# GpSimd instead of SyncE issues the reads that bring regrouped token tiles back, in a gated convolution and neighbourhood attention encoder

## The chip, the cores and the metric

One core of one Trainium2 chip. The metric is the device time of one execution in microseconds (us), lower is better. The kernel before took 1714.12 us, the median of 3 runs (1713.75 to 1716.57).

## The reference

One encoder layer and a final RMSNorm for two requests with the same weights, 512 and 1024 tokens of 1024 channels, all in float32. The part that the change touches is the first two lines.

```python
def _layer(x, norm_g, w_in, b_gate, dw_w, dw_b, ln_g, ln_b, w_pw_a, rpb, w_o_b, w_out):
    proj = _rmsnorm(x, norm_g) @ w_in
    a_val, a_glu, z_a, q, k, v, z_b, g_logits = jnp.split(proj, np.cumsum(sizes)[:-1].tolist(), axis=-1)
    y_a = (_conv_module(a_val, a_glu, dw_w, dw_b, ln_g, ln_b) * jax.nn.silu(z_a)) @ w_pw_a
    attn = _neighbourhood_attention(q.reshape(hs), k.reshape(hs), v.reshape(hs), rpb)
    y_b = (attn * jax.nn.silu(z_b)) @ w_o_b
    gates = jax.nn.sigmoid(g_logits + b_gate)
    merged = gates[..., :D_MODEL] * y_a + gates[..., D_MODEL:] * y_b
    return x + merged @ w_out
```

## The kernel before

The 1536 tokens are 12 tiles of 128. Every float32 operand of a matrix product is split into a high and a low part, and each product is three passes on TensorE (PE in the profile). The normalised and transposed activations stay in SBUF as `xs` (high and low), the weights come piece by piece.

**The first phase** (up to about 83 us) does two things at once. It normalises and transposes the 12 tiles, and it multiplies each finished tile with the first half of the V weights: one group of 24 matmuls per tile (`token_group`, the matmul of L1675). PE works through the tiles in order, so tile t has to be in `xs` when the group of tile t - 1 ends. After that come the conv groups (L1657), the other V half, Q and K, and the attention units, all with `xs` complete.

How a tile gets into `xs`:

- SyncE (SP) loads it (`load_x`, L502); ScalarE squares and sums it (`square`, L843); VectorE scales the sum (`mean_square_x`, L1221); GpSimd (POOL) takes the power -1/2 (L729), in a loop over the 12 tiles, each behind a wait for `ms_ok`.
- Tiles 0 to 4: VectorE multiplies (`normalise`, L1235), PE transposes (`h_t`, L1695).
- Tiles 5 to 11 (from `SHUFFLED`) leave PE alone: VectorE multiplies and turns the tile in blocks of 32 x 32 (`turn`, four of L1246 and the transpose L1249, into one of two buffers `xn`), and SP moves the blocks through DRAM (`shuffle_x`): four stores to `x_d` (L521), a wait until they have landed, one read of 512 KB back into `xt` (L523).
- All tiles: ScalarE copies the high part (`h_hi`, L858, two halves; for tiles 5 to 11 it waits for the read by `x_back`), VectorE subtracts for the low part (`h_lo`, L1261, two halves), and `x_lo` lets PE go on.

ScalarE's program has `h_hi(t + 1)` ahead of `take_v(t)`, which empties PE's group t (L871) and issues its store (L874). VectorE's has `h_lo(t)` ahead of `turn(t + 3)`.

**SP's order** in `shuffle_x`, in one queue: tile 5 before the load of tile 11, then tiles 6 to 11, then the window masks (L532), the small parameters (L535, into the buffer of the odd `xn`) and the weight pieces of the second V half (L494).

**The semaphores**: `xr_ok` counts the turned tiles, `x_out` the stores (64 for a tile), `x_back[t % 2]` the reads (16 each). `turn(t)` waits on `x_out` until the stores of tile t - 2, which used the same buffer, are done.

**GpSimd after the loop** waits for the whole `xs` (`x_lo` at 24), clears a small table, loads the position bias and writes it as a shifted table to DRAM (L735, L739: 16 DMAs), then builds the masked biases (L759) that attention takes.

Of the kernel before, what the change touches and what calls it, by code (L numbers as in the profile page):

```python
# [104 lines left out]
SHUFFLED = 5  # L105
# [86 lines left out]
def build(nc, x_prompt, x_sample, norm_g, w_in, b_gate, dw_w, dw_b, ln_g, ln_b, w_pw_a, rpb,  # L192
          w_o_b, w_out, final_g, masks, y_prompt, y_sample):
    with ExitStack() as ctx:
# [3 lines left out]
        def sem(name):  # L198
            return ctx.enter_context(nc.semaphore(name))

        def scratch(name, shape):
            return nc.dram_tensor(name, shape, F32, kind="Internal").ap()
# [30 lines left out]
        xt = work[:, 0:8 * D].rearrange("p (s d) -> p s d", s=8)  # L233
# [33 lines left out]
        def wt(s, part):  # L267

            return spare[:, part, :] if wslot(s) == X_SLOT else ws[:, wslot(s), part, :]
# [43 lines left out]
        x_d = scratch("x_d", [NT, P, 4, 2 * P])  # L313
# [12 lines left out]
        table0, rel_out = sem("table0"), sem("rel_out")  # L326
        mask_ok, pads_ok = sem("mask_ok"), sem("pads_ok")
        sq_ok, ms_ok, rstd_ok, xn_ok, ht_ps = (sem(n) for n in ("sq_ok", "ms_ok", "rstd_ok", "xn_ok", "ht_ps"))
        xp_ok, xr_ok, x_out, x_back = sem("xp_ok"), sem("xr_ok"), sem("x_out"), [sem(f"x_back{i}") for i in range(2)]
        x_hi, x_lo, x0_hi, x0_lo = sem("x_hi"), sem("x_lo"), sem("x0_hi"), sem("x0_lo")  # L330
        w_ld = [sem(f"w_ld{i}") for i in range(2)]
        w_ld2 = [sem(f"w_ld2{i}") for i in range(2)]
# [51 lines left out]
        def w_rows(w, col, s):  # L384

            return w.rearrange("(k p) c -> p k c", p=P)[:, 2 * s:2 * s + 2, col:col + CH]
# [28 lines left out]
        def grs(g):  # L415

            return g % 2, g + 1, g // 2 + 1
# [61 lines left out]
        def after(eng, sm, count):  # L479

            if not isinstance(count, int) or count > 0:
                eng.wait_ge(sm, count)
# [5 lines left out]
        def _(sp):  # L488
# [26 lines left out]
            def shuffle_x(t):  # L515

                sp.wait_ge(xr_ok, t - SHUFFLED + 1)
                spot = x_d[t].rearrange("(g i) a n -> a i g n", g=4)
                for a in range(4):
                    src = xn[t % 2][32 * a:32 * a + 32, :].rearrange("p (g n) -> p g n", g=4)  # L520
                    sp.dma_start(spot[a], src).then_inc(x_out, 16)  # L521
                sp.wait_ge(x_out, 64 * (t - SHUFFLED + 1))
                sp.dma_start(xt[:, t % 8, :], x_d[t].rearrange("p a n -> p (a n)")).then_inc(x_back[t % 2], 16)  # L523

            for t in range(8, NT):
                load_x(t)
# [1 line left out]
                    shuffle_x(t - 5)  # L528
            for t in range(7, NT):
                shuffle_x(t)  # L530
            sp.wait_ge(w_lo, 4)
            sp.dma_start(msk32, masks).then_inc(mask_in, 16)  # L532
            for r, n, src in ((0, TAPS, dw_w[0]), (I_DWB, 1, dw_b[0:1, :]), (I_LNG, 1, ln_g[0:1, :]),
# [135 lines left out]
            for e in range(2 * 24):  # L669
                ct, n = (e % 24) // NCH, e % NCH  # L670
                if e >= 3:

                    b, _, out = grs(G_YB + e - 3)
# [19 lines left out]
            for j in range(6, 8):  # L693
                src = w_rows(w_out[0], CH, j - 4)
# [7 lines left out]
            for e in range(4, 2 * NT):  # L702
                b, _, out = grs(G_OUT + e - 4)
# [10 lines left out]
        @block.gpsimd  # L714
        def _(pool):
            nc.gpsimd.memset(ident[:], 0.0).then_inc(const_ok, 1)
            nc.gpsimd.memset(half, -0.5).then_inc(const_ok, 1)
            pool.wait_ge(const_ok, 2)
            nc.gpsimd.affine_select(out=ident[:], in_=ident[:], compare_op=ALU.not_equal, fill=1.0, base=0,
                                    pattern=[[-1, P]], channel_multiplier=1).then_inc(const_ok, 1)  # L720
            for t in range(NT):
                if t == 1:

                    pool.wait_ge(w_hi, 1)
                    pool.wait_ge(xn_ok, 2)
                    nc.gpsimd.tensor_tensor(wt(0, 1), raw_of(0), wt(0, 0).bitcast(F32), ALU.subtract).then_inc(w_lo, 1)

                pool.wait_ge(ms_ok, t + 1)
                nc.gpsimd.tensor_tensor(rstd[:, t:t + 1], ssq[:, t:t + 1], half, ALU.pow).then_inc(rstd_ok, 1)  # L729

            pool.wait_ge(x_lo, 3 * KT)
            nc.gpsimd.memset(table[0:HEADS, :], 0.0).then_inc(table0, 1)
            pool.wait_ge(table0, 1)
            t3 = table[0:HEADS, :].rearrange("h (r c) -> h r c", r=RROWS)
            pool.dma_start(t3[:, 4:4 + 15, 16:16 + 31], rpb[0]).then_inc(tab_in, 16)  # L735
            pool.wait_ge(tab_in, 16)
            for c in range(QB):

                pool.dma_start(rel_d[:, c, :, :], t3[:, :, 15 - c:15 - c + ECOLS]).then_inc(rel_out, 16)  # L739
            pool.wait_ge(mask_ok, 1)  # L740

            def unit(i):
                for kd in range(KINDS):
                    for h in range(2):
                        s, jk = kd // 3, kd % 3
                        j = JKIND.index(jk)
                        nk = SEG_ROWS[s] * 8 * QUADS[j]
                        if kd == 0:
                            pool.wait_ge(e_in[h], 128 * i + 128)

                        used = 0 if kd < 2 else blk(0, 4 * ((kd - 2) // 3) + [0, 2, 3][(kd - 2) % 3], h)
                        after(pool, t_ok, 24 * i + used)
                        e0 = 16 - QB * j + BAND_START[j]
                        e = et[h][:, SEG_E0[s]:SEG_E0[s] + SEG_ROWS[s], e0:e0 + 8 * QUADS[j]]
                        if QUADS[j] == 3:
                            e, w = e.rearrange("p r (v w) -> p v r w", v=3), 8
                        else:
                            e, w = e.rearrange("p (c g) w -> p g c w", g=4), BAND
                        nc.gpsimd.tensor_tensor(  # L759
                            bt[:, 2 * (kd % 2) + h, 0:nk].rearrange("p (g c w) -> p g c w", g=QUADS[j], w=w),  # L760
                            mask[:, KIND_OFF[kd]:KIND_OFF[kd] + nk].rearrange("p (g c w) -> p g c w", g=QUADS[j], w=w),
                            e, ALU.subtract).then_inc(bias_ok, 1)

            unit(0)
            with pool.Fori(1, PAIRS) as i:
                unit(i)


            pool.wait_ge(c_out, 32 * PAIRS)
            for k in range(KT):  # L770

                pool.wait_ge(x_lo, 5 * KT + k + 1 if k < KT - 2 else 6 * KT)
                if k >= 3:
                    pool.wait_ge(dev, k - 2)
                pool.dma_start(cs[:, k, :], c_d[k]).then_inc(c_in[k], 16)

            pool.wait_ge(var_ok, 1)
            nc.gpsimd.tensor_tensor(var, var, half.to_broadcast([P, NT]), ALU.pow).then_inc(rcol_ok, 1)

            def load_za(e):  # L780
                n, k = e // KT, e % KT
                pool.dma_start(tmp3[:, chunk(e % 3)], za_d[k, :, chunk(n)]).then_inc(za_in[e % 3], 16)


            pool.wait_ge(sum_ps, 2 * NCH + 1)
            for n in range(3):
                pool.wait_ge(st_out[n], 128 + 48 * PAIRS)
            for e in range(3):
                load_za(e)
            for e in range(3 * KT):  # L790
                n, k = e // KT, e % KT
                pool.wait_ge(lw, e + 1)
                pool.wait_ge(za_in[e % 3], 16 * (e // 3 + 1))
                nc.gpsimd.tensor_tensor(cs[:, k, chunk(n)], cs[:, k, chunk(n)], tmp3[:, chunk(e % 3)],
                                        ALU.mult).then_inc(ta_ok, 1)
                if e + 3 < 3 * KT:
                    pool.wait_ge(ta_ok, e + 1)
                    load_za(e + 3)

            for t in range(NT):  # L800
                pool.wait_ge(fms, t + 2 + t // (NT - 1))
                nc.gpsimd.tensor_tensor(rsf[:, t:t + 1], rstd[:, t:t + 1], half, ALU.pow).then_inc(frs, 1)
# [399 lines left out]
        def _(dve):  # L1202
# [34 lines left out]
            def turn(t):  # L1237

                dve.wait_ge(rstd_ok, t + 1)
                n = t - SHUFFLED  # L1240
                after(dve, x_out, 64 * (n - 1))
                src = xt[:, t % 8, :].rearrange("p (k g i) -> p k g i", k=KT, g=4)
                dst = xn[t % 2].rearrange("p (g k i) -> p k g i", g=4, k=KT)
                g = ngb.rearrange("p (k g i) -> p k g i", k=KT, g=4)
                for q in range(4):
                    nc.vector.scalar_tensor_tensor(dst[:, :, q, :], src[:, :, q, :], rstd[:, t:t + 1], g[:, :, q, :], ALU.mult,  # L1246
                                                   ALU.mult).then_inc(xp_ok, 1)
                dve.wait_ge(xp_ok, 4 * n + 4)
                nc.vector.transpose(xn[t % 2], xn[t % 2]).then_inc(xr_ok, 1)  # L1249
# [309 lines left out]
            for phase, e0, s0 in ((2, 0, S_YB), (3, 24, S_YA)):  # L1559
                for gi in range(24):  # L1560
                    tile, n = gi // NCH, gi % NCH
# [38 lines left out]
            for e in range(2 * NT):  # L1600
                c, t = e // NT, e % NT
# [4 lines left out]
                b, done, _ = grs(G_OUT + e)  # L1606
# [351 lines left out]
```

## Time and profile before

| | |
|---|---|
| median of 3 runs | 1714.12 us |
| the profiled execution | 1714.49 us |
| its span | 1712.7 us |
| PE busy | 1701.9 us, 99% of the span |
| VectorE busy | 1154.4 us, 67% |
| ScalarE busy | 463.9 us, 27% |
| GpSimd busy | 186.3 us, 11% |
| DMA | 237.57 MB, 139 GB/s on average |

The span is the time from the first to the last instruction; the profiled execution's own time is 1.79 us more. PE is busy nearly all the time, so what matters is how long it waits and where; matmuls are pipelined and their ends are modelled, so that a short wait can hide inside a busy stretch and shows in the spacing of the groups.

### The profile page before, as it was taken

To read this page: it belongs to the slowest core of one execution; us is meant where nothing else is said; L and a number is where in the kernel's file an instruction comes from. 1 tells how busy PE (TensorE), PEld (TensorE's weight loads), DVE (VectorE), ACT (ScalarE), POOL (GpSimd) and SP (SyncE) were. 2 spreads that over 40 slices of the span, in tenths; PEclk is the share of its full clock that TensorE was granted. 3 is DMA by queue.
4 is the path that set the end of the run, shared out by engine and by line. 5 is a ranking of instruction groups with operands and counts; after the bars stand their busy time and mean duration, and the time that the engine had idled before them with its cause. 6 is when DMAs were issued, how large, how long until landed. Compare 5 with 4: busy or idle time off the path is not lost.

```text
span 1712.7 us, 25348 instructions
## 1 busy us (share of the span) xinstructions
PE 1701.9 (99%) x8644; PEld 1404.3 (82%) x8644; DVE 1154.4 (67%) x1875; ACT 463.9 (27%) x931; POOL 186.3 (11%) x251
## 2 busy tenths in 40 slices
PE   9999999999999999999999999999999999999998
PEld 7788888888888888888888888888887888888887
DVE  6549256896798589579678958967986655335332
ACT  5321123223122222222222222231234344003222
POOL 1120011001011001001101100010110064000001
PEclk9999999999999999999999999999999999999999
DMA  8751345444435434534543553453458675643223
GB/s 299 236 95 50 97 122 137 122 118 138 130 88 157 110 106 124 157 90 118 152 122 82 146 138 103 115 146 112 131 149 313 229 223 164 199 130 105 76 91 130
DMA packets 281286, 237.57 MB, mean 139 GB/s; under 512 B 106040, under 2 KB 235080, under 8 KB 281069
## 3 DMA queue, kind: packets, MB, share of 16 engines
q1 hardware_dynamic: 231818, 147.01, 30.7%
q10 hardware_dynamic: 45506, 75.78, 13.3%
q0 software_dynamic: 3872, 13.75, 3.0%
q8 instruction: 38, 0.62, 0.2%
q14 instruction: 52, 0.42, 0.1%
HBM read 152.75 MB, written 83.71 MB: 138 GB/s over the span
## 4 chain that ended last, share of the span: by engine, by line
PE 93%; DMA 3%; DVE 2%; SPq 1%; issue 1%; ACT 0%; ACTq 0%; POOL 0%; POOLq 0%; DVEq 0%
PE pg L1657 74%; PE pg L1675 12%; PE pS L1834 2%; PE pS L1815 2%; DMA x_d<-work 1%; PE pO L1834 1%; PE pO L1815 1%; DMA work<-in_norm_g 1%; DVE xs L1214 1%; SPq L521 0%; DMA work<-p_d 0%; DMA p_d<-work 0%; DMA m_d<-work 0%; PE pS L1792 0%; DMA work<-x_d 0%
## 5 line engine op out<-in xcount | busy, mean ns | idle before, releaser
L1657 PE MATMUL pg<-xs,ws 128*128 128x512 f32 x5688 | 1303.8, 390 | 0.2 <-DVE work L1555 0.2
L1657 PEld LDWEIGHTS pg<-xs,ws 128*128 128x128 f32 x5688 | 1064.1, 188 | 228.2 <-issue 6.4
L1328 DVE SCALAR_TENSOR_TENSOR work<-work 128x1551 f32<-128x1551 f32 x240 | 439.1, 1830 | 16.8 <-issue 12.0
L1675 PE MATMUL pg<-ws,xs 128*128 128x512 f32 x942 | 218.7, 390 | 0.8 <-DVE xs L1261 0.8
L1675 PEld LDWEIGHTS pg<-ws,xs 128*128 128x128 f32 x942 | 176.4, 188 | 38.2 <-issue 1.7
L759 POOL TENSOR_TENSOR work<-work 128x288 f32<-128x288 bf16 (+3 forms) x72 | 53.5, 742 | 976.3 <-DVE small L1401 964.0
L1052 ACT ACTIVATE work<-work,small 128x288 f32<-128x288 f32 (+3 forms) x192 | 102.7, 537 | 200.9 <-DVE small L1401 200.9
L1206 DVE TENSOR_TENSOR ws<-raw,ws 128x1024 fp32r<-128x1024 f32 x88 | 109.2, 1242 | 54.1 <-ACT ws L812 54.1
L812 ACT ACTIVATE ws<-raw 128x1024 fp32r<-128x1024 f32 x89 | 93.9, 1056 | 127.5 <-PE pg L1657 99.2
L1401 DVE CUSTOM_DVE_ANT_0 work<-pS,work 128x384 f32<-128x384 f32 (+3 forms) x128 | 53.3, 463 | 95.7 <-PE pS L1815 94.6
L1413 DVE STREAM_TRANSPOSE work<-work 128x288 f32<-128x288 f32 (+3 forms) x192 | 94.0, 490 | 6.6
L1411 DVE TENSOR_SCALAR work<-work,small 128x288 f32<-128x288 f32 (+3 forms) x192 | 90.1, 469 | 6.8
L1025 ACT ACTIVATE work<-pg,work 128x512 f32<-128x512 f32 x48 | 33.1, 689 | 163.3 <-PE pg L1657 158.7
L1551 DVE SCALAR_TENSOR_TENSOR work<-qk,pg 128x512 f32<-128x512 f32 x24 | 16.5, 687 | 73.0 <-PE pg L1657 73.0
L759 POOL TENSOR_TENSOR work<-work,ws 128x288 f32<-128x288 bf16 (+3 forms) x72 | 56.2, 780 | 68.6 <-DMA ws<-rel_d 68.6
L1625 DVE TENSOR_TENSOR work<-pg,work 128x512 f32<-128x512 f32 x23 | 15.9, 691 | 59.2 <-PE pg L1675 59.2
L1360 DVE TENSOR_TENSOR ws<-pg,qk 128x512 fp32r<-128x512 f32 x24 | 16.5, 689 | 49.4 <-ACT qk L914 49.4
L1214 DVE SCALAR_TENSOR_TENSOR xs<-work,xs 128x512 fp32r<-128x512 f32 x69 | 43.1, 686 | 8.9 <-ACT xs L965 8.9
L914 ACT ACTIVATE qk<-pg 128x512 fp32r<-128x512 f32 x24 | 14.4, 599 | 118.5 <-PE pg L1657 118.5
L1834 PEld LDWEIGHTS pS<-work 128*64 128x64 f32 (+1 forms) x672 | 34.4, 136 | 11.3 <-issue 11.3
L965 ACT ACTIVATE xs<-work 128x512 fp32r<-128x512 f32 x69 | 38.0, 621 | 20.4 <-DVE work L1547 9.1
L920 ACT ACTIVATE qk<-pg 128x512 fp32r<-128x512 f32 x24 | 14.4, 598 | 105.9 <-PE pg L1657 105.9
(142 smaller groups left out, 1023.4 us busy)
## 6 DMA issues: line engine op xcount, KB each, us to landing
raw<-in_w_in SPq DMA_DIRECT2D x70, 512.0 KB, 3.8
p_d<-work SPq DMA_DIRECT2D x128, 96.0 KB, 2.1
work<-p_d ACTq DMA_DIRECT2D x32, 384.0 KB, 3.6
p_d<-work SPq DMA_DIRECT2D x128, 72.0 KB, 1.9
work<-p_d ACTq DMA_DIRECT2D x31, 288.0 KB, 3.7
v_d<-work ACTq DMA_DIRECT2D x24, 256.0 KB, 2.6
work<-v_d SPq DMA_DIRECT2D x64, 96.0 KB
za_d<-work ACTq DMA_DIRECT2D x24, 256.0 KB, 2.1
```

The lines of the kernel that those rows point to most:

```text
L759: nc.gpsimd.tensor_tensor(bt[:, 2 * (kd % 2) + h, 0:nk].rearrange("p (g c w) -> p g c w", g=QUADS[j], w=w), mask[:, KIND_OFF[kd]:KIND_OFF[ ...
L812: nc.scalar.activation(wt(s, 0), raw_of(s), ACT.Copy).then_inc(w_hi, 1)
L1052: nc.scalar.activation(t, t, ACT.Exp, scale=-1.0, bias=mn[:, x:x + 1], accum_out=rsum[:, x:x + 1]).then_inc(p_exp, 1)
L1206: nc.vector.tensor_tensor(wt(s, 1), raw_of(s), wt(s, 0).bitcast(F32), ALU.subtract).then_inc(w_lo, 1)
L1214: nc.vector.scalar_tensor_tensor(xs[:, k, 1, chunk(n)], src_of(k), scale, xs[:, k, 0, chunk(n)].bitcast(F32), ALU.mult, ALU.subtract).then ...
L1328: nc.vector.scalar_tensor_tensor(cv[:, 0:CLEN], u[:, k:k + CLEN], cur[:, k:k + 1], cv[:, 0:CLEN], ALU.mult, ALU.add).then_inc(tap_ok, 1)
L1401: nc.vector.tensor_tensor_reduce(out=head_of(tt, b, h), in0=bank_of(b, h)[:, 0:nk], in1=bt[:, 2 * (kind_of(b) % 2) + h, 0:nk], scale=1.0, ...
L1411: nc.vector.tensor_scalar(t, t, rinv[:, x:x + 1], None, ALU.mult).then_inc(p_ok, 1)
L1413: nc.vector.transpose(t, t).then_inc(tr_done, 1)
L1657: last = nc.tensor.matmul(pg[b][:], wt(s, wpart)[:, k * P:(k + 1) * P], xs[:, k, xpart, chunk(n)], start=(j == 0 and wpart == 1), stop=(j ...
L1675: last = nc.tensor.matmul(pg[b][:], xs[:, k, xpart, t * P:(t + 1) * P], wt(s0 + k // 2, wpart)[:, chunk(k % 2)], start=(k == 0 and xpart = ...
L1834: mm = nc.tensor.matmul(o[:, a:z], vb[0:rows_of(b), SEG_RG[s] + c, j, rows], p[:, c, a:z], start=(n == 0), stop=(n == nc_ - 1))
```

## The change

SP no longer waits for its stores and no longer reads the tiles back. GpSimd does, in its loop over the tiles: after the power of tile 6 it waits for the stores of tile 5 and issues the read of tile 5, and so on by a small table; the reads of tiles 9, 10 and 11 all come after the last power. The stores are counted by two semaphores, for odd and even tiles. New on SP is a wait before the stores of tile t until the read of tile t - 2 has landed, and one for all stores before the masks.

```diff
-        xp_ok, xr_ok, x_out, x_back = sem("xp_ok"), sem("xr_ok"), sem("x_out"), [sem(f"x_back{i}") for i in range(2)]
+        xp_ok, xr_ok, x_out, x_back = sem("xp_ok"), sem("xr_ok"), [sem(f"x_out{i}") for i in range(2)], [sem(f"x_back{i}") for i in range(2)]
...
             def shuffle_x(t):
 
                 sp.wait_ge(xr_ok, t - SHUFFLED + 1)
+                after(sp, x_back[t % 2], 16 * ((t - SHUFFLED) // 2))
...
-                    sp.dma_start(spot[a], src).then_inc(x_out, 16)
-                sp.wait_ge(x_out, 64 * (t - SHUFFLED + 1))
-                sp.dma_start(xt[:, t % 8, :], x_d[t].rearrange("p a n -> p (a n)")).then_inc(x_back[t % 2], 16)
+                    sp.dma_start(spot[a], src).then_inc(x_out[t % 2], 16)
...
+            for i, n in ((0, 3), (1, 4)):
+                sp.wait_ge(x_out[i], 64 * n)
             sp.wait_ge(w_lo, 4)
...
+            def load_back(t):
+
+                pool.wait_ge(x_out[t % 2], 64 * ((t - SHUFFLED) // 2 + 1))
+                pool.dma_start(xt[:, t % 8, :], x_d[t].rearrange("p a n -> p (a n)")).then_inc(x_back[t % 2], 16)
...
                 nc.gpsimd.tensor_tensor(rstd[:, t:t + 1], ssq[:, t:t + 1], half, ALU.pow).then_inc(rstd_ok, 1)
+                for b in {6: (5,), 8: (6,), 9: (7,), 10: (8,), 11: (9, 10, 11)}.get(t, ()):
+                    load_back(b)
...
-                after(dve, x_out, 64 * (n - 1))
+                after(dve, x_out[t % 2], 64 * (n // 2))
```

SP's queue before, from the stores of tile 5 to those of tile 7. `x_d<-work` is a store (4 for a tile), `work<-x_d` the read, `work<-in_x_sample` the load of tile 11.

```order
L521 DMA x_d<-work 32x4x256 [waits xr_ok]
L521 DMA x_d<-work 32x4x256 x3
L523 DMA work<-x_d 128x1024 [waits x_out]
L502 DMA work<-in_x_sample 128x1024 [waits ht_ps]
L521 DMA x_d<-work 32x4x256 [waits xr_ok]
L521 DMA x_d<-work 32x4x256 x3
L523 DMA work<-x_d 128x1024 [waits x_out]
L521 DMA x_d<-work 32x4x256 [waits xr_ok]
```

SP's queue with the change, from the stores of tile 5 to those of tile 8:

```order
L522 DMA x_d<-work 32x4x256 [waits xr_ok]
L522 DMA x_d<-work 32x4x256 x3
L502 DMA work<-in_x_sample 128x1024 [waits ht_ps]
L522 DMA x_d<-work 32x4x256 [waits xr_ok]
L522 DMA x_d<-work 32x4x256 x3
L522 DMA x_d<-work 32x4x256 [waits x_back1,xr_ok]
L522 DMA x_d<-work 32x4x256 x3
L522 DMA x_d<-work 32x4x256 [waits x_back0,xr_ok]
```

The reads and their waits are gone, the load of tile 11 follows the stores of tile 5 at once, and from tile 7 on the stores wait for the read of two tiles before.

GpSimd's program with the change, from the power of tile 1 (the first row is that of tiles 1 to 6) to the clearing of the table:

```order
L735 TENSOR_TENSOR small<-small 128x1 [waits ms_ok] x6
L725 DMA work<-x_d 128x1024 [waits x_out1]
L735 TENSOR_TENSOR small<-small 128x1 [waits ms_ok] x2
L725 DMA work<-x_d 128x1024 [waits x_out0]
L735 TENSOR_TENSOR small<-small 128x1 [waits ms_ok]
L725 DMA work<-x_d 128x1024 [waits x_out1]
L735 TENSOR_TENSOR small<-small 128x1 [waits ms_ok]
L725 DMA work<-x_d 128x1024 [waits x_out0]
L735 TENSOR_TENSOR small<-small 128x1 [waits ms_ok]
L725 DMA work<-x_d 128x1024 [waits x_out1]
L725 DMA work<-x_d 128x1024 [waits x_out0]
L725 DMA work<-x_d 128x1024 [waits x_out1]
```

Before, the eleven powers of tiles 1 to 11 stood in one row with nothing between them; now the powers of tiles 7, 9, 10 and 11 stand behind a read and its wait.

## Rows read from the trace of the kernel before

**Rows 1.** Waits of PE in the whole span: us in total, times, longest us
```profile
PE pg L1702 <- POOL ident L719: 1.6, 1, 1.6
...
PE pg L1675 <- DVE xs L1261: 0.8, 2, 0.5
```
**Rows 2.** PE's L1675, groups of tiles 8 to 11: length, then busy (count)
```profile
59.54:64.98 5.44, 5.40 (x24) 4.13 (x22) 1.00 0.74 238
64.98:70.97 5.99, 5.72 (x24) 4.43 (x24) 1.00 0.70 222
70.97:77.18 6.21, 5.76 (x25) 4.72 (x26) 1.00 0.77 262
77.18:82.67 5.49, 5.45 (x24) 4.13 (x23) 1.00 0.66 248
```
**Rows 3.** ScalarE and PE around tile 10: start us, length us, line [idle before]
```profile
69.91 1.16 ACT L858 ACTIVATE xs<-work 128x512 fp32r<-128x512 f32 x2 [4.33 <-DMA work<-x_d]
...
71.42 11.21 PE L1675 MATMUL pg<-ws,xs 128*128 128x512 f32 x48 [0.52 <-DVE xs L1261]
```
**Rows 4.** SP's DMA issues from 29 to 75 us: start, length
```profile
33.79 0.34 SPq L523 DMA_DIRECT2D work<-x_d  x1
...
46.45 0.34 SPq L523 DMA_DIRECT2D work<-x_d  x1
...
53.58 1.88 SPq L521 DMA_DIRECT2D x_d<-work  x4
59.36 0.34 SPq L523 DMA_DIRECT2D work<-x_d  x1
...
66.07 2.33 SPq L521 DMA_DIRECT2D x_d<-work  x4
71.27 0.34 SPq L523 DMA_DIRECT2D work<-x_d  x1
71.65 0.43 SPq L532 DMA_DIRECT2D work<-in_masks  x1
```
**Rows 5.** Median us from issue to landing: 30 to 90 us, then two later stretches
```profile
work<-x_d SPq DMA_DIRECT2D x7, 512.0 KB, 4.1
...
work<-za_d POOLq DMA_DIRECT2D x24, 256.0 KB, 3.8
qk<-gb_d SPq DMA_DIRECT2D x10, 256.0 KB, 4.0
...
work<-c_d POOLq DMA_DIRECT2D x8, 768.0 KB, 7.5
raw<-in_w_o_b SPq DMA_DIRECT2D x4, 512.0 KB, 5.6
```
**Rows 6.** A wait of GpSimd and the DMA issue behind it, in a later phase
```profile
1388.92 0.58 POOL L782 DMA_DIRECT2D work<-za_d  x1 [0.30 <-POOL work L794]
```
**Rows 7.** GpSimd's powers of tiles 7, 9 and 11: start, length [idle before]
```profile
35.23 0.55 POOL L729 TENSOR_TENSOR small<-small 128x1 f32<-128x1 f32 x1 [4.73 <-DVE small L1221]
...
46.70 0.55 POOL L729 TENSOR_TENSOR small<-small 128x1 f32<-128x1 f32 x1 [5.88 <-DVE small L1221]
...
56.59 0.55 POOL L729 TENSOR_TENSOR small<-small 128x1 f32<-128x1 f32 x1 [4.87 <-DVE small L1221]
```
**Rows 8.** VectorE's turn of a tile: the multiplications of 11, the transposes of 9 and 11
```profile
49.80 1.25 DVE L1249 STREAM_TRANSPOSE work<-work 128x1024 f32<-128x1024 f32 x1
...
59.44 1.67 DVE L1246 SCALAR_TENSOR_TENSOR work<-work,small 128x256 f32<-128x256 f32 x4
61.15 1.25 DVE L1249 STREAM_TRANSPOSE work<-work 128x1024 f32<-128x1024 f32 x1
```
**Rows 9.** GpSimd's first use of the odd heads' table, read back from DRAM
```profile
185.50 0.56 POOL L759 TENSOR_TENSOR work<-work,ws 128x192 f32<-128x192 bf16 x1 [68.63 <-DMA ws<-rel_d]
```
**Rows 10.** VectorE with two SBUF inputs, and a read issued by GpSimd meanwhile
```profile
1327.39 1.75 DVE L1511 TENSOR_TENSOR work<-work 128x1536 f32<-128x1536 f32 x1
1327.44 0.53 POOL L775 DMA_DIRECT2D work<-c_d  x1 [2.40 <-DVE work L1511]
```

## The prediction

> **What bounds the kernel now.** I read the waits of TensorE first: it waits next to never, and over the whole span only 0.8 us of its waits are on `h_lo`, the last step of bringing a token tile into `xs` [rows 1]. These two waits lie in the groups of tiles 9 and 10. So the change can give back little, whatever it does to SyncE.
>
> A short wait can hide in the modelled ends of matmuls, so I read the spacing of the groups too, in windows cut at the starts of ScalarE's copies out of PSUM. The group of tile 8 takes 5.44 us for 24 matmuls; tiles 9, 10 and 11 take 5.99, 6.21 and 5.49 [rows 2]. The excess is 0.55 + 0.77 + 0.05 = **1.37 us**, all that PE loses to late tiles.
>
> Third, the row of what makes tile 10 late: ScalarE sat idle for 4.33 us until the read from `x_d` landed, started at 69.91, and PE could go on at 71.42 [rows 3]. From landing to PE's start are 1.51 us (half a tile on ScalarE, then on VectorE).
>
> Fourth, why the read is late. SP does everything of one tile in one chain: stores, a wait, the read, and only then the next stores. The stores of tile 9 start at 53.58 and its read at 59.36, that is 5.78 us; for tile 11 it is 66.07 to 71.27, 5.20 us [rows 4]. From the read of tile 9 at 59.36 to that of tile 11 at 71.27 are 6.0 us a tile [rows 4], and PE needs 5.44, so the lead shrinks with every tile until it is gone. VectorE had finished turning tile 9 at 51.05 and tile 11 at 62.40 [rows 8], but their stores went out at 53.58 and 66.07 [rows 4]: 2.5 and 3.7 us of waiting in SP's queue.
>
> **The change, part by part.** Let L be the time from the passing of GpSimd's wait to the landing of its read. SP's reads of this size land in 4.1 us in this very stretch [rows 5]. Whether GpSimd's do is not in the trace. Bounds: its reads of 256 KB take 3.8 us, those of 768 KB 7.5 us, in a stretch where SP's 512 KB take 5.6 [rows 5]. Like against like, 256 KB take 3.8 us from GpSimd and 4.0 from SP [rows 5], so I take SP's 4.1 for the transfer and add the 0.30 us that GpSimd spends between a wait and the issue behind it [rows 6]: **L = 4.4 us**, ends 3.8 and 7.5.
>
> *The odd tiles*, now in two queues. GpSimd may read tile 7 only after the power of tile 9, which ends at 46.70 + 0.55 = 47.25, about 47.3 [rows 7]; its stores had landed at 46.45 even in SP's old queue [rows 4]. It lands at 47.3 + 4.4 = 51.7. The stores of tile 9 wait for that (the new wait on SP) and for the turn at 51.05 [rows 8]: they start at 51.7, against 53.58, and have landed 5.8 us later, 57.5. The last power ends at 57.14 [rows 7], so the read of tile 9 is not held up: it lands at 61.9. The stores of tile 11 go at 61.9, land at 67.7, and its read lands at 72.1.
>
> *What PE needs*: without stalls its groups would begin at 64.98 (tile 9), 70.42 and 75.86, and the reads have to land 1.51 us ahead: 63.5, 68.9 and 74.35. The margins are 1.6 us for tile 9 and 2.2 for tile 11. *The even tiles* are easier: the power of tile 10 lies half way between those of 9 and 11 [rows 7], at about 51.6, so the read of tile 8 lands at about 51.6 + 0.6 + 4.4 = 56.6; tile 10 is turned by then (half way between 51.05 and 62.40), its stores have landed at 62.4 and its read lands at 66.8, a margin of 2.1. So all three stalls go: **-1.37 us**.
>
> In terms of L: tile 9 lands at 53.1 + 2L and is in time up to L = 5.2; tile 11 lands at 58.9 + 3L, so PE's loss is 3L - 15.45 from L = 5.15 on. It equals today's 1.37 at L = 5.6, and is 3.4 us more (0.2%) at L = 6.75. Every later figure comes from this line.
>
> *What comes behind GpSimd's waits* are the powers. That of tile 7 started at 35.23 [rows 7] and now stands behind the wait for the stores of tile 5, over at 33.79 [rows 4], plus 0.30 and an issue of 0.58 [rows 6]: 34.67, still ahead. If the stores land 1 us later, the power is 0.4 us late and so are the turn and the stores of tile 7; they had landed at 46.45 [rows 4] and are not needed before 47.3. The power of tile 9 stands behind the stores of tile 6, landed one SP round of 6 us before 46.45; that of tile 10 (about 51.6) behind those of tile 7, 46.45; that of tile 11 (56.59) behind those of tile 8, landed a round before 59.36. All are over 3 us early. Cost 0; without that cover a late power would move the turn of its tile by as much.
>
> *The load of tile 11* no longer waits on SP for the stores of tile 5, and shares the DMA engines with the read of tile 5. Bound: 0 to the 1.5 us between 4.1 and the 5.6 of a crowded stretch [rows 5]. PE takes up tile 5 at 64.98 - 4 x 5.44 = 43.22 and needs it landed by 41.7; crowded, it lands at 33.79 + 0.3 + 5.6 = 39.7. Cost 0.
>
> *The masks*: SP issued them (1280 KB) right behind the read of tile 11, at 71.65 [rows 4]. Now SP waits only for the stores and issues them at 67.7, in another queue than that read and at the same moment. They are the one big competitor that is new. Bounds for that read: L = 4.4 if it is not touched, 7.5 if it goes like the crowded reads of 768 KB. Nearest is 512 KB in the crowded stretch, 5.6 [rows 5]: 73.3 + 0.3 = 73.6 against 74.35. No loss, with 0.7 us in hand; at 7.5 a loss of 0.85.
>
> *The two semaphores* change no wait of VectorE: it still waits for the stores of tile t - 2. *Downstream*, the seven reads stand in GpSimd's queue ahead of the table's DMAs, which may land some us later. Covered: GpSimd uses the second table at 185.50, after a wait of 68.63 us [rows 9]. Cost 0; without that cover PE's first scores would be late by the same. Everything behind the first phase is bound by PE and moves forward with it.
>
> **The sum**, against the profiled execution of 1714.49 us (span 1712.7 plus 1.79 around it): 1714.49 - 1.37 = 1713.12 us. The median of the runs shown is 0.37 us lower, so 1714.12 - 1.37 = 1712.75: **1712.8 us**.
>
> **A rule weighed against a row.** A GpSimd read issued while VectorE was 0.05 us into a two-input operation of 1.75 us took 0.53 us to issue [rows 10], about the 0.58 of an ordinary one [rows 6]: in this row VectorE does not hold GpSimd's issue up. The Trainium skill speaks against the change at this point: "SBUF — State Buffer", section "SBUF: two separate sides", says that while VectorE is in a two-port mode GpSimd is locked out of the port it writes descriptors through, and advises SP's or ScalarE's queue. Its section "Who interferes with whom" counts copies, casts and tensor_scalar among these operations; two inputs only hold up GpSimd's reads. By that rule the sum would stay, as long as only one-element ones of these run beside the seven issues.
>
> **The rivals.**
>
> *1. The reads are slower from GpSimd, but not by much* (L from 5.2 to 6.75). For: half way between 3.8 and 7.5 is 5.65, and the 7.5 was taken on this queue; the reads now run beside the next stores, not ahead of them. Against: the 7.5 belongs to a crowded stretch, where SP's 256 KB are slow too. At 5.6 the time is unchanged, 1714.1; at 6.75 it is 1717.5. A late masks collision alone gives 1713.6. Chance 0.22.
>
> *2. Slower: VectorE holds up the making of the descriptors.* The place is VectorE's turn of a tile, four multiplications of 1.67 us together and a transpose of 1.25 [rows 8], 2.92 us; if the transfer can only start after them, L = 4.4 + 2.9 = 7.3. The loss is 3 x 7.3 - 15.45 = 6.45, that is 5.1 more than now: 1719.2 us. It decides from L = 6.75, a delay of 2.35 us. Against it stands the issue of 0.53 us under a 1.75 us operation [rows 10]; for it, that none of GpSimd's transfers in the trace was issued beside a transpose, and that an issue's length is not the transfer's start. This is the case that the skill's warning would be, if it held for more operations than it lists. Chance 0.06.
>
> *3. The handover changes nothing*: SP's queue is freed, but what follows is set by VectorE's turns, each of which stands behind `h_lo` of three tiles before, and PE still waits. At the old rate for the last two tiles, 1714.1. Against: turned tiles lay 2.5 to 3.7 us in SP's queue. Chance 0.04.
>
> *4. Faster by more than 3.4 us*: PE would have to be losing more in the first phase than the groups show; all its other waits are at the start [rows 1]. Chance 0.02.
>
> **How the numbers follow.** The forecast has 0.66. About 0.2% (3.4 us) is what a measurement of this kernel can tell from no change; the three runs span 2.8 us. Within it lie the forecast, rival 3 and rival 1: 0.66 + 0.04 + 0.22 = 0.92. Slower: 0.06. Faster: 0.02. The range reaches down to 1711.2, the forecast less half the spread of the runs, and up over rival 1 to L = 6.2, where the loss is 3.15 and the time 1715.9, plus 0.3: 1716.2. It leaves out rival 2, rival 4 and the tail of rival 1.
>
> **What would show it.** In the changed kernel's profile: the groups of tiles 9 to 11 at 5.44 us each; no wait of PE on `h_lo`; SP's wait for each tile's stores gone; stores of tile 9 near 51.7 and of tile 11 near 61.9; GpSimd's reads near 47.3, 57.5 and 67.7 and landing in 4 to 5 us; ScalarE's start on tile 11 near 72 to 73.6; the masks issued near 68. I am wrong in L if the landings are over 5.2 us, and in the premise if the landings are as expected and the groups still take over 5.9.

## The result and the profile after

The changed kernel takes **1721.47 us**, the median of 6 runs (1717.75 to 1723.72), against 1714.59 us of six runs of the kernel before. The ratio is 1.0037, 95% interval 1.0027 to 1.0047: slower by 0.4%, 6.3 us by the ratio and 6.9 by the medians, where 1.4 us less was forecast. It also scatters more: 6.0 us between its fastest and its slowest run, 4.2 for the kernel before.

The profiled execution happens to be the fastest of the six (1717.75 us, span 1715.9). Its waits of PE, to set beside [rows 1]:

```profile
PE pg L1683 <- DVE xs L1269: 4.0, 3, 3.0
PE pg L1710 <- POOL ident L720: 1.6, 1, 1.6
PE pg L1718 <- ACT ws L820: 1.4, 1, 1.4
```

Everything is as before except the wait on `h_lo`: 4.0 us in place of 0.8. Its three waits are for tile 7 (0.4 us), tile 10 (0.6) and tile 11 (3.0). The spacing of PE's groups says the same more fully. These windows are cut like those of [rows 2], tiles 7 to 11:

```profile
53.72:59.84 6.12, 5.77 (x25) 4.80 (x26) 1.00 0.94 260
59.84:65.28 5.44, 5.40 (x24) 4.13 (x22) 1.00 0.70 200
65.28:71.25 5.97, 5.72 (x24) 4.43 (x24) 1.00 0.76 201
71.25:80.00 8.75, 5.73 (x24) 4.42 (x24) 1.00 0.82 304
80.00:86.17 6.17, 5.68 (x24) 4.43 (x24) 1.00 0.30 80
```

Five groups in 32.45 us where five times 5.44 are 27.20: 5.25 us lost, against 1.37 before. (The cut at 80.00 stands near the end of PE's wait for tile 11, not at the end of the group of tile 10, because ScalarE waited for the same read before it made that copy. The sum is not touched by it.) That is 3.9 us more than before. PE came to these groups 0.4 us earlier (53.72 against 54.10), so the last of them ended at 86.17 instead of 82.67, 3.5 us later. The span is 3.2 us longer: the whole loss of this execution lies in the first phase.

What made PE wait is in the chain that ended last. It is shown for the changed kernel from the power of tile 9 on (start us, length us, what):

```profile
46.33 0.52 POOL small L735
46.85 5.70 DMA work<-x_d
...
52.61 0.30 SPq L522
...
53.92 4.26 DMA x_d<-work
58.17 0.29 issue
58.46 5.36 DMA work<-x_d
...
63.88 0.30 SPq L522
...
65.19 5.33 DMA x_d<-work
70.52 0.28 issue
70.80 8.12 DMA work<-x_d
78.92 0.02 issue
78.95 0.64 ACT xs L866
79.61 0.70 DVE xs L1269
```

This is the chain of the odd tiles that the prediction wrote down, link by link, with other durations: reads of 5.7, 5.4 and 8.1 us where 4.1 was taken, and the last one started at 70.8 where 67.7 was reckoned. The stores of tile 11 are slower too: 6.6 us from their first issue at 63.88 to the landing of the last at 70.52, where 5.8 was taken and the kernel before needed 5.2 [rows 4]. Medians from issue to landing from 30 to 90 us, beside [rows 5]:

```profile
work<-x_d POOLq DMA_DIRECT2D x7, 512.0 KB, 5.7
x_d<-work SPq DMA_DIRECT2D x27, 128.0 KB, 2.7
```

The reads have become slower (4.1 before). A single store has become faster in the median, 2.7 us against 3.9, but the read waits for the last of four, and those of tile 11 took 2.0, 2.7, 4.7 and 5.3 us. And the last read was issued next to the masks, and had still not landed when SP had issued all the parameters and a piece of weights:

```profile
70.57 0.35 SPq L533 DMA_DIRECT2D work<-in_masks  x1
...
72.94 0.40 SPq L494 DMA_DIRECT2D raw<-in_w_in  x1
```

### The profile page after: what moved, and what is told of

It reads as the page before. It is cut to its first block, busy times and chain, and to the rows that moved or that the text cites. A ratio compares the mean times of both kernels' runs of the same rounds, so it can differ in the third digit from the quotient of the medians.

```text
span 1715.9 us, 25354 instructions
## 1 busy us (share of the span) xinstructions
PE 1702.0 (99%) x8644; PEld 1404.4 (82%) x8644; DVE 1153.5 (67%) x1875; ACT 464.6 (27%) x931; POOL 190.5 (11%) x258
## 4 chain that ended last, share of the span: by engine, by line
PE 94%; DMA 3%; DVE 1%; issue 1%; ACT 1%; SPq 0%; POOL 0%; ACTq 0%; POOLq 0%; DVEq 0%
PE pg L1665 74%; PE pg L1683 12%; PE pS L1842 2%; PE pS L1823 2%; DMA work<-x_d 1%; PE pO L1842 1%; PE pO L1823 1%; DMA x_d<-work 1%; DVE xs L1222 1%; PE pg L1718 1%; PE pg L1710 0%; DMA work<-p_d 0%; DMA p_d<-work 0%; PE pS L1800 0%; DMA m_d<-work 0%
```

## The experiments

Three theories to start with. **A**: the read of tile 11 collides with the masks, the parameters and the weight pieces. **B**: GpSimd's reads are slow, and SP's new wait hands each delay on. **C**: the rest of the loss lies behind the first phase. All times are beside runs of the kernel before on the same chip. In the diffs `...` stands for what is left out.

**1. The changed kernel again.** No edit.

> The changed kernel once more, for a second profile: the profiled execution was the fastest of its six (1717.75 against a median of 1721.47), so some 4 us of the loss stand in no trace yet. Theory A (the read of tile 11 collides with the masks, the parameters and the weight pieces): in a slower execution the read of tile 11 takes still longer than 8.1 us and PE's wait ahead of its group is about 3 + 4 us. Theory B (all of GpSimd's reads are slow, and each delay passes through SP's new wait to the next but one tile): the reads of tiles 7 and 9 land later too and PE waits for tiles 9 and 10 as well. Theory C: the 4 us lie behind the first phase, at a place that these two do not touch.

Measured: 1720.19 us, ratio 1.0044 (1.0030 to 1.0058); the profiled execution was the median one. Theory C falls: PE's wait on `h_lo` is now 6.3 us in five waits, 5.5 us more than before the change, and the span 5.7 us longer.

```profile
PE pg L1683 <- DVE xs L1269: 6.3, 5, 2.6
```

```profile
47.01 6.48 DMA work<-x_d
...
54.86 5.17 DMA x_d<-work
60.03 0.29 issue
60.32 5.43 DMA work<-x_d
...
67.13 6.26 DMA x_d<-work
73.40 0.28 issue
73.68 7.80 DMA work<-x_d
```

Again the same chain (these are rows of its chain of waits): the last read is no slower than in the faster run, 7.8 us, but it starts 2.9 us later. The 2.9 us are links of this chain: the read of tile 7 took 0.8 us more, the stores of tiles 9 and 11 took 0.9 us more each, and the rest is the start. So the delays pass from tile to tile, as theory B has it, but the stores carry more of this difference than the reads. That the scatter of the other executions has the same origin is likely, and no trace shows it.

**2. The masks after the reads.**

```diff
             for i, n in ((0, 3), (1, 4)):
                 sp.wait_ge(x_out[i], 64 * n)
+            for i, n in ((0, 3), (1, 4)):
+                sp.wait_ge(x_back[i], 16 * n)
```

> The changed kernel, but SP waits for all reads to land before it issues the masks, the parameters and the weight pieces. Theory A: the last read lands in about 5.5 us in place of 8.1, PE's wait ahead of tile 11 falls from 3.0 to under 0.7 us, time 1714.5 to 1716. Theory B: the reads of tiles 9 and 10 stay late, so at most 2.5 us come back, 1719. Theory C: no change, 1721.5.

Measured: 1716.97 us, ratio 1.0020 (1.0011 to 1.0029). By the ratios 4.1 us come back of 7.5 (by the medians 3.2 of 6.3), between what A and B expected. The read of tile 11 is now the shortest of all:

```profile
74.24 0.53 POOL L727 DMA_DIRECT2D work<-x_d  x1 [5.58 <-DMA x_d<-work]
```

```profile
78.26 1.15 ACT L868 ACTIVATE xs<-work 128x512 fp32r<-128x512 f32 x2 [2.73 <-DMA work<-x_d]
```

Issued at 74.24 and taken up at 78.26: **4.0 us with neither masks nor stores of a tile beside it** (only a store of 256 KB to `v_d`, from 75.56), against 7.8 and 8.1 beside the masks. The other reads are as slow as ever (median 5.9), and PE still waits 3.8 us in this profile, now for tiles 7 to 10.

**3. Without the new wait of SP.** Seven semaphores for the reads in place of two, so that two reads never count on the same one.

```diff
-        ... [sem(f"x_back{i}") for i in range(2)]
+        ... [sem(f"x_back{i}") for i in range(7)]
-                after(sp, x_back[t % 2], 16 * ((t - SHUFFLED) // 2))
-                pool.dma_start(...).then_inc(x_back[t % 2], 16)
+                pool.dma_start(...).then_inc(x_back[t - SHUFFLED], 16)
-                act.wait_ge(x_back[t % 2], 16 * ((t - SHUFFLED) // 2 + 1))
+                act.wait_ge(x_back[t - SHUFFLED], 16)
```

> The changed kernel without SP's wait for the read of two tiles before (seven semaphores for the reads in place of two, so that none is shared). Theory B: the stores of tiles 9 and 11 leave 1.5 and 2 us earlier, and with them the read of tile 11: 2 to 3 us faster, 1718.5 to 1719.5. Theory A: the read of tile 11 and the masks both move forward together and still collide: the gain is the 1 to 2 us of the earlier start, 1720. Rival: the wait kept reads and stores apart, and without it both land later: same or slower.

Measured: 1715.54 us, ratio 1.0009 (1.0000 to 1.0018), some 5 to 6 us back, more than either theory expected.

```profile
PE pg L1682 <- DVE xs L1268: 1.9, 2, 1.6
```

The read of tile 11 is issued at 65.80 and, beside the masks (10.5 us themselves), takes 10.4 us, longer than in any other run; but it starts 5.0 us earlier than in the first profile and lands at 76.3. Of the 5.0 us, 2.7 are the earlier start of the stores of tile 11 (61.18 in place of 63.88) and 2.3 their landing, 4.3 us in place of 6.6. So without the wait the stores do not only leave earlier, they also land sooner.

**4. ScalarE issues the reads**, for tiles 5 to 9 within 1.5 us of the moments at which GpSimd did. SP's new wait stays, and so does the place of the masks.

```diff
-                for b in {6: (5,), 8: (6,), 9: (7,), 10: (8,), 11: (9, 10, 11)}.get(t, ()):
-                    load_back(b)
...
+                    if SHUFFLED <= t + 2 < NT:
+                        load_back(t + 2)
                     take_v(t)
```

> The changed kernel, but ScalarE issues the seven reads, within about 1 us of the moments at which GpSimd did (ahead of its copy of the group two tiles before). Only the queue differs. Theory B, that GpSimd's queue makes the reads slow: they land in about 4.1 us in place of 5.7, also that of tile 11, and PE's waits go: 1713. Theory A (what runs beside them makes them slow, whatever the queue): 5 to 6 us and about 8 for the last, 1719 to 1721.

Measured: 1713.67 us, ratio 1.0001 (0.9992 to 1.0010), so all of the loss is gone. PE does not wait on `h_lo` at all in its profile. The reads and the stores of this kernel:

```profile
x_d<-work SPq DMA_DIRECT2D x28, 128.0 KB, 4.0
...
work<-x_d ACTq DMA_DIRECT2D x7, 512.0 KB, 4.7
```

4.7 us, and 6.6 for the last one beside the masks (issued at 67.89, the read at 67.86): less than from GpSimd, but not SP's 4.1. The read of tile 9 took 4.8 us with the stores of tile 10 issued 1.1 us ahead of it, where GpSimd's took 5.4 with these 1.0 us ahead. So neither "it is the queue" nor "it is what runs beside it" is the whole answer yet.

**5. Both mends together**, with the reads left to GpSimd: the edits of 2 and 3.

> The two mends together: no wait of SP for reads before the stores, and the masks, parameters and weight pieces only when all reads have landed. GpSimd's queue is kept. If the loss is made of the coupling and of the collision alone, PE's wait on h_lo goes to about 0.3 us and the time to 1713.5 to 1714.5, as with the reads on ScalarE (1713.67). If GpSimd's queue has a price of its own beyond these two (a read of 5.4 us beside stores, where ScalarE's took 4.7), some 1 us stays: 1715.

Measured: 1714.31 us, ratio 1.0000 (0.9990 to 1.0009). PE does not wait on `h_lo` in its profile, and the copy out of the last group starts at 81.36, against 82.67 before. So the loss goes without undoing GpSimd as the issuer. Its reads still take 5.4 us in the median, which the chain without the coupling (SP's new wait) absorbs. The coupling alone left 1.0020 (experiment 2) and the collision alone 1.0009 (experiment 3). Both act on how long a read takes: experiment 4 leaves them in place and makes the reads shorter, and the loss goes as well.

**6. The read of tile 7 ahead of the power of tile 9.**

```diff
-                for b in {6: (5,), 8: (6,), 9: (7,), 10: (8,), 11: (9, 10, 11)}.get(t, ()):
+                for b in {6: (5,), 8: (6, 7), 10: (8,), 11: (9, 10, 11)}.get(t, ()):
```

> The changed kernel with one entry moved: the read of tile 7 stands before the power of tile 9, not behind it. The prediction let the chain of the odd tiles start at 47.3 us, at that power. If the chain is that of the odd tiles, its start moves to about 45 us and the reads of tiles 9 and 11 come up to 2 us earlier: 1718 to 1719. If the reads and the even tiles' stores slow each other down anyway, under 1 us comes back, 1720; the power of tile 9 may even be late behind the wait.

Measured: 1719.09 us, ratio 1.0031 (1.0019 to 1.0044); against 1.0037 and 1.0044 the intervals overlap, so a gain is not shown. In the profile the read of tile 7 leaves at 44.99 in place of 46.85 and that of tile 11 at 69.32 in place of 70.80, and it still meets the masks, issued at 69.08. An earlier start of the chain moves both of them.

**7. The masks ahead of the last read, in the kernel before.** No GpSimd reads; SP issues the masks between the stores of tile 11 and the wait for them, and no longer behind the read.

```diff
+                if t == NT - 1:
+                    sp.wait_ge(w_lo, 4)
+                    sp.dma_start(msk32, masks).then_inc(mask_in, 16)
                 sp.wait_ge(x_out, 64 * (t - SHUFFLED + 1))
```

> The kernel before, but SP issues the masks (1280 KB) between the stores of tile 11 and the wait for them, so that the read of tile 11 comes behind them in SP's own queue. It measures the collision without GpSimd. If big transfers in flight cost a read 2 to 4 us on any queue: tile 11's read lands in 6 to 8 us in place of 4.1, PE waits 2 to 3 us more, 1716 to 1717. If only GpSimd's queue suffers: 1714.

Measured: 1718.50 us, ratio 1.0038 (1.0025 to 1.0052): **as slow as the change itself**, with one DMA moved up. (The medians lie 3.8 us apart, the ratio stands for 6.5: three of the five runs lie at 1717.7 to 1718.5, two at 1722.6 and 1722.9.) The rows of PE's wait, of SP and of ScalarE:

```profile
PE pg L1676 <- DVE xs L1262: 3.8, 3, 2.6
```

```profile
69.14 0.49 SPq L524 DMA_DIRECT2D work<-in_masks  x1
...
72.35 0.34 SPq L526 DMA_DIRECT2D work<-x_d  x1
```

```profile
79.03 1.15 ACT L859 ACTIVATE xs<-work 128x512 fp32r<-128x512 f32 x2 [6.64 <-DMA work<-x_d]
```

6.7 us from issue to use on SP's own queue, 2.5 more than before. The stores of tile 11 had also left 0.9 us later than in the kernel before (66.92 against 66.07), which is no effect of the masks. The collision does not need GpSimd; the kernel before avoids it by the order of its issues [rows 4], where the masks come 0.4 us behind the read.

**8. SP keeps the reads, one tile behind.** The read of tile t - 1 is issued after the stores of tile t; one semaphore for each read.

```diff
                     sp.dma_start(spot[a], src).then_inc(x_out[t % 2], 16)
+                if t > SHUFFLED:
+                    load_back(t - 1)
+                if t == NT - 1:
+                    load_back(t)
```

> A version that could beat both: SP keeps the reads, but issues the read of tile t - 1 behind the stores of tile t, so that it never idles until stores land; one semaphore for each read. Stores of tiles 9 and 11 leave 2 to 4 us earlier than before, reads stay in the order of one queue. All three stalls go: 1.4 us faster than before, 1712.5. Rival: reads and the next stores now overlap and slow each other, the reads take 5 us and more, and the gain is under 0.5 us.

Measured: 1714.61 us, ratio 0.9999 (0.9990 to 1.0008): no gain, as the rival of the expectation has it, though its reads were to take 5 us and more.

```profile
work<-x_d SPq DMA_DIRECT2D x7, 512.0 KB, 4.7
x_d<-work SPq DMA_DIRECT2D x27, 128.0 KB, 2.5
```

The reads took 4.7 us as from ScalarE, with the next stores now ahead of them in the same queue, and PE waited 0.6 us on `h_lo`. The last read took 6.2 us although the masks were issued 0.5 us behind it; the read of tile 10 was still in flight when it left, so standing ahead of the masks is no full protection. The 1.4 us to be had are less than this measurement can tell.

**9. No store of a tile beside a read.** SP holds the stores of each tile back until the read of the tile before has landed.

```diff
-                after(sp, x_back[t % 2], 16 * ((t - SHUFFLED) // 2))
+                if t > SHUFFLED:
+                    sp.wait_ge(x_back[(t - 1) % 2], 16 * ((t - 1 - SHUFFLED) // 2 + 1))
```

> The changed kernel with SP's stores of each tile held back until the read of the tile before has landed, so that no read runs beside a store of a tile. It is much slower by construction (a round of stores, read and handover of some 9.5 us against PE's 5.44 for six tiles: 15 to 20 us more than the kernel before); what it measures is the landing of GpSimd's reads, beside VectorE's turns but without stores. If what runs beside a read makes it slow, all seven land in 4.0 to 4.3 us, like SP's in the kernel before. If GpSimd's queue, or VectorE holding up its descriptors, makes them slow, they stay at 5.4 to 6.2 us.

Measured: 1735.51 us (two runs), ratio 1.0125 (1.0106 to 1.0143), 21 us slower than the kernel before. What counts are the landings, 30 to 110 us:

```profile
work<-x_d POOLq DMA_DIRECT2D x7, 512.0 KB, 4.0
```

and one of these reads beside a whole turn of a tile on VectorE:

```profile
62.78 1.67 DVE L1255 SCALAR_TENSOR_TENSOR work<-work,small 128x256 f32<-128x256 f32 x4 [2.54 <-DMA x_d<-work]
62.98 0.57 POOL L726 DMA_DIRECT2D work<-x_d  x1 [5.29 <-DMA x_d<-work]
64.49 1.25 DVE L1258 STREAM_TRANSPOSE work<-work 128x1024 f32<-128x1024 f32 x1
67.00 1.15 ACT L867 ACTIVATE xs<-work 128x512 fp32r<-128x512 f32 x2 [5.46 <-DMA work<-x_d]
```

Issued at 62.98 and taken up at 67.00, 4.0 us, through all four multiplications and the transpose. Without stores of a tile beside them five of GpSimd's seven reads took 3.8 to 4.1 us, as SP's did; that of tile 6 took 4.8, and the last, beside the masks, 7.5. VectorE's turn did not hold this read up. Nor is it needed for a slow one: in the changed kernel the read of tile 10 (64.31 to 70.16) took 5.9 us, and VectorE was idle but for the 1.3 us of `h_lo`.

**10. ScalarE's reads with the masks after them.** The edits of 4 and 2 together.

> Reads issued by ScalarE, and the masks, parameters and weight pieces only after the last read. The reads of ScalarE alone took PE's waits away already, so this should change nothing that PE sees: 1713 to 1714, within 0.1% of the kernel before; the read of tile 11 should fall from 6.6 to 4.1 us. If something behind the first phase were waiting for the masks, it would show here as slower than 1714.5.

Measured: 1713.88 us, ratio 0.9996 (0.9987 to 1.0005). The last read was issued at 67.61 and taken up at 71.06, 3.4 us. The time does not rise, so nothing behind the first phase that PE depends on waits for the masks.

## Why the prediction was wrong

- **What bounds the kernel, and what there is to gain: right.** PE loses 1.37 us to late tiles. Where the waits on `h_lo` are gone (experiments 4 and 5) the kernel is at ratios of 1.0001 and 1.0000, with intervals of 0.0009 to either side: no gain is shown, and one of 1.4 us could not be told from none. In single profiles it shows: the five groups from 53.57 us on in that of experiment 10 take 27.20 us, five times 5.44, and the span is 1711.3 us against 1712.7. The chain of the odd tiles was the right one as well; the trace shows it link by link.
- **The step that failed is L, "so I take SP's 4.1 for the transfer".** It was to be 4.4 us with the handover. Measured are 5.7 and 6.2 as medians of the two profiles, without the 0.3. The 4.1 us of [rows 5] were not the price of a read that runs alone. Right behind the read of tile 9, issued at 59.36 [rows 4], SP issued the stores of tile 10:

```profile
59.74 3.09 SPq L521 DMA_DIRECT2D x_d<-work  x4
```

The read stood 0.4 us ahead of them in the same queue and landed in 4.3 us. With the change, the stores of the next tile go out on SP's queue ahead of the read or beside it, and GpSimd sends the read. Neither of the two makes the price by itself. GpSimd's reads without these stores took 4.0 us (experiment 9), and reads of ScalarE and SP with the stores ahead of them or beside them took 4.4 to 4.7 in the median (experiments 4, 8 and 10). The two together gave 5.4 to 6.2. The prediction carried the price of the old order and of the old issuer into the new kernel.

- **The masks: named, and mis-sized.** The text gave 5.6 us for the read beside them, 7.5 as the bad end. It was 8.1 and 7.8 (7.5 in experiment 9, 6.7 on SP's own queue in experiment 7). The nearest row was taken from a crowded stretch of equals; here 1280 KB of masks and 512 KB of weights came on top. I had the row against it (the reads of 768 KB at 7.5) and put it aside. The prediction also let this case stand alone, at 1713.6, so that it cost 0.85 us: but it met a tile that was late already, and then each us of it is a us of PE.
- **The formula 3L - 15.45 was too mild.** With L = 5.7 + 0.3 it gives a loss of 2.55 us, where the groups show 5.25. The last read adds 2.4 us (8.1 + 0.3 against 6.0). The stores of tile 11 add 0.9: from the landing of the read of tile 9 to their own are 6.7 us, where the sum has 5.8 from the kernel before. The other links were 1.3 us shorter than the formula has them at this L, so that the last read landed 2.0 us later than by the formula. PE wanted it 0.4 us earlier than in the kernel before, and its last group took 0.3 more.
- **The even tiles and tile 7 were closer than the text has it.** A read that lands late delays `h_lo`, and VectorE's turn of three tiles later stands behind that; this was mentioned for rival 3 and not put into the sum. The trace shows it for tile 10: `h_lo` of tile 7 waited for a read that landed at 52.55, the turn of tile 10 ended at 57.40 where 56.7 was reckoned, its stores took 6.6 us and its read landed at 70.2, not at 66.8. It did not act on the chain of the odd tiles: tile 11 was turned at 61.74, and its stores waited until 63.88 for the read of tile 9. For tile 7 no margin was given. PE needed its read by 54.10 - 1.51 = 52.59, only 0.9 us behind the 51.7 of the text, and it waited for this tile as well.
- **Rival 1 had the mechanism ("the reads now run beside the next stores, not ahead of them"), with too short a reach and 0.22.** At the measured L of 6.0 to 6.5 (with the 0.3) its line gives 1715.3 to 1716.8. It ended at 1717.5 because L and the masks were never late together, and because the stores kept their 5.8 us.
- **Rival 2 had the sign, with a wrong cause.** VectorE's turn did not hold up GpSimd's read (experiment 9). The Trainium skill's warning ("SBUF — State Buffer", section "SBUF: two separate sides") lists two-port modes alone, and the trace agrees as far as it goes: 4.0 us through a turn. Of the operations that the prediction names for it (copies, casts, tensor_scalar) only the scaling of the sum, one element for each partition and 0.1 us long, ran beside reads of the changed kernel, so no run here tests the warning itself.
- **Powers, load of tile 11, two semaphores for VectorE, table: cost 0, right as far as is seen.** The read of tile 5, beside the load of tile 11, took 6.2 us, over the bound of 5.6, and landed at 39.8, well before the 41.7 at which it was needed. The power of tile 7 starts at 34.87 in place of 35.23. None of them appears in the chain, apart from the power of tile 9 at its start, as foreseen.
- **The range.** By its own working the lower end is 1712.75 - 1.41 = 1711.3, not 1711.2; nothing hangs on it. The upper end, 1716.2, left out L above 6.2 and the collision on top of it.

How the loss splits, by the ratios: the changed kernel is 7.5 us slower in experiment 1 (1.0044). The masks after the reads give back 4.1 us (to 1.0020), no coupling 6.0 (to 1.0009), both together all (1.0000), and ScalarE as the issuer all as well (1.0001). These do not add up, since they are links of one chain: what one saves becomes slack that absorbs the other.

Open is why GpSimd's reads beside stores (5.4 us in experiment 5) take longer than ScalarE's or SP's (4.7 in 4 and 8, 4.4 in 10). The moments of issue differ by up to 2 us and ScalarE's reads share a queue with its stores to `v_d`; no run isolates it. The Trainium skill, "DMA: Bandwidth & Descriptors", section "Queues, rings and completion order", says that a DMA engine takes packets in turn from each queue that has work. That would agree with reads slowed by stores in another queue. But 4.7 us from SP's own queue in experiment 8 shows that separate queues are not needed for it, and the stores do not follow the number of queues either: 4.0 us in the median with the reads on ScalarE's queue (experiment 4), 2.5 with both on SP's (experiment 8).

## What to carry to other kernels

A landing time belongs to the order in which it was measured, and to the issuer. Where a change makes an issuing engine stop waiting, transfers that stood behind another one now stand ahead of it or beside it. Price them by rows with that order and that issuer. Look also at what the freed queue will issue next: here SP sent 1280 KB of masks, which could wait for the last read without any loss (experiment 10), beside the one read that PE was about to wait for. In a chain whose links feed each other, put all the late cases in together; one at a time each fits in the slack.

## What the runs showed of the hardware that was not expected

- A read of 512 KB from DRAM took 4.0 us in the median from GpSimd without a tile's stores beside it (experiment 9), and 4.1 from SP with 512 KB of stores 0.4 us behind it in the same queue (the kernel before). With such stores ahead of it or beside it, it took 4.7 (SP in experiment 8), 4.4 and 4.7 (ScalarE in 10 and 4) and 5.4 to 6.2 (GpSimd). Beside 1280 KB of masks and what follows them it took 6.6 (ScalarE), 6.7 (SP), 7.5 to 8.1 and once 10.4 (GpSimd).
- One DMA of 1280 KB issued 3.2 us ahead of a needed read, in place of 0.4 us behind it, took that read from 4.1 to 6.7 us; the kernel became 0.38% slower by the ratio (experiment 7).
- The median of single stores says little of when a tile is out in DRAM. A single store took 2.7 us in the median of the changed kernel, and the four of tile 11 needed 6.6 us, against 5.2 in the kernel before with a median of 3.9.
